# State-space scan of a two-block model: each head's decay sums are repeated on 128 partitions by transfers from DRAM instead of by selection products

## The chip, the cores and the metric

The kernel runs on one core of one Trainium2 chip. Its engines are TensorE (PE in the profile, with its weight loads as PEld), VectorE (DVE), ScalarE (ACT), GpSimd (POOL) and SyncE (SP), which here only issues DMA transfers. Sixteen DMA engines move data between DRAM and the on-chip memory SBUF; TensorE writes its results to the eight banks of PSUM. The metric is the time of one execution on the device in microseconds, as the median of several runs.

## The reference, cut to what matters

The reference computes two blocks on 512 tokens of width 1024. The first block has a state-space branch (32 heads in 4 groups, forward and backward over the sequence), a pooling branch and a mixture of 32 experts; the second has attention, a recurrence and two feed-forward layers. The change lies in the chunked scan of the first block:

```python
def step(state, inp):                      # one chunk of q = 128 tokens
    xc, ac, bc, cc = inp
    acs = jnp.cumsum(ac, axis=1)
    seg = acs[:, :, None] - acs[:, None, :]
    decay = jnp.exp(jnp.where(lower, seg, -jnp.inf))
    cb = jnp.einsum('bign,bjgn->bijg', cc, bc)
    y_diag = jnp.einsum('bijg,bijgr,bjgrp->bigrp', cb, decay, xc)
    ...
```

`acs` is the running sum of the decay within a chunk, for each of 32 heads and 2 directions. The matrix `seg` needs, for every pair of tokens (i, j) of a chunk, the sum at i minus the sum at j. The kernel holds j on the 128 partitions and i along the free dimension, for four chunks side by side (512 columns). The sum at j is then one number per partition, but the row of sums at i has to stand on all 128 partitions. How this row gets there is what is changed.

## The kernel before, in words

Every engine has its own program, written as Python functions with the engine's name in front (`pe_scan`, `act_scan`, `dve_scan`); semaphores tie them together. `x.next(key)` marks an instruction, `wait_ge(*x.when(key))` waits for it. Each engine runs its instructions in the order in which they are written out.

**Where the sums are.** `acs2` holds them with the token on the partition, each twice. TensorE transposes them (L1054 to L1060), so that row hh of the result (hh = 32 d + 8 g + h for direction d, group g, head h) holds the 512 sums of one head and direction. ScalarE copies all 128 rows to `ats` rounded to float32r (L2052), VectorE replaces the lower 64 by the rest that the rounding left (L2646, called at L2806), and ScalarE makes a table `oneh` of selection columns.

**The heads.** The scan goes through four groups of eight heads. In a group, six chunks of the input projection are made and convolved ("wxbc" weights), then four state steps run, then the eight heads one after another. `pe_decayed(g, h)` selects row hh of `ats` onto all partitions of a PSUM bank, once per direction: two matmuls of 512 columns (L1014). `act_decayed` turns the backward bank into the exponent of the decay, in four ACTIVATE instructions (L1981) written to `E4[h % 2][0]`; `dve_decayed` does it with the forward bank, in four TENSOR_SCALAR instructions (L2743) written to `E4[h % 2][1]`, and then merges the two with a copy under a mask (L2748). `act_exponential` (L1987) takes the exponential, VectorE multiplies by C·B (L2923), and TensorE multiplies with the head's inputs (L1145).

**What is woven in.** After each head, `gap(1, True)` lets two other streams go on. The `filler` is half a weight tile's products for z and the gates ("wz", "wg", later "wu"), 12 matmuls of 512 columns (L851 to L853). The result goes through `FB` to a DRAM scratch (`spill`, L1917 and L1919, 256 KB). The `later` stream is one tile of the second modulation matrix ("wada", L940), and every fourth time a turn (L950). On ScalarE the order in a head is: `act_decayed` of the next head, the exponential, and then the filler's part. That is the high half of a coming weight tile (`hi`, L502) or a spill.

**Weight tiles.** SyncE loads them, 512 KB each, into four slots (`raw`), in the order in which TensorE takes them (L460). A tile of "wz", "wg", "wxbc" or "wu" is split by ScalarE into a high part (L502) and by VectorE into a low part (L513), and its slot is free after the low part. A "wada" tile is used as it is, and its slot is free when TensorE has used it. `Plan` fixes in advance which slot each tile gets and at which point it is split, some tiles ahead of its use (AHEAD = 4). In the heads of groups 0 to 2 the order is two "wada", one "wz" or "wg", and so on. For example, the first "wada" after tile wz 11 gets the slot of wz 11, the second that of an earlier "wada".

## Time and profile before

| | |
|---|---|
| median of 3 runs | 2458.35 us (2451.48 to 2459.67) |
| the profiled execution | 2453.99 us, its span 2452.6 us |
| TensorE busy | 2379.8 us, 97% of the span |
| VectorE, ScalarE, GpSimd busy | 65%, 46%, 15% |
| chain that ended last | PE 75%, DMA 10%, DVE 8%, ACT 5% |
| SyncE's queue (q1) | 377.42 MB, 41.5% of the 16 DMA engines' time |
| ScalarE's queue (q10) | 25.17 MB, 2.8% |
| selection products (L1014) | 64, from 189.9 to 651.4 us |

The span is one execution as the hardware profiler saw it. A share is the busy time over that span, and a mean over stages that have different limits: in the expert stage (slices 16 to 22 of 40) the DMA engines are full, in the scan TensorE is. The chain is followed back from the last instruction to what released each step.

### The profile page before, as it was taken

The page shows a single profiled execution, that of the slowest core. Times are in us where ns is not written, and L with a number is a line of the kernel's source. Part 1 is how long each engine was busy: PE and PEld are TensorE (multiplying, and loading weights), DVE is VectorE, ACT ScalarE, POOL GpSimd, SP SyncE. Part 2 cuts the span into 40 slices and gives each one's busy share as a digit, 9 for nine tenths or more (in the row PEclk, how much of TensorE's full clock was granted, in tenths as well). Part 3 has the DMA queues.
Part 4 walks back from the last instruction along what each step waited for, and adds up shares of the span by engine and source line. Part 5 has one row for each costly group of instructions (what it writes and reads, how often), then busy time and mean ns, then how long its engine had stood idle before and what let it go on. Part 6 is the DMA issues. An engine that isn't in the chain of part 4 may idle for free.

```text
span 2452.6 us, 34034 instructions
## 1 busy us (share of the span) xinstructions
PE 2379.8 (97%) x13716; PEld 1913.7 (78%) x13716; DVE 1586.6 (65%) x2352; ACT 1134.8 (46%) x1690; POOL 357.8 (15%) x324
## 2 busy tenths in 40 slices
PE   6999999999899999999999989999999999999999
PEld 3876868677777877777666678989988777889988
DVE  2676676868645667655555677667753677667666
ACT  2424434343445446655555574434353546534433
POOL 0010111202232311111111110100032000201110
PEclk9999999999999999999999999999999999999999
DMA  7315234242346369999999934767542111567763
GB/s 273 116 60 182 93 126 145 87 140 96 129 154 221 119 218 384 424 423 423 423 422 423 373 130 133 168 163 185 113 144 77 44 43 52 155 147 180 174 156 109
DMA packets 127043, 467.83 MB, mean 191 GB/s; under 512 B 17194, under 2 KB 27690, under 8 KB 101153
## 3 DMA queue, kind: packets, MB, share of 16 engines
q1 hardware_dynamic: 91488, 377.42, 41.5%
q0 software_dynamic: 21952, 63.01, 12.2%
q10 hardware_dynamic: 13440, 25.17, 2.8%
q8 instruction: 110, 1.80, 0.3%
q14 instruction: 53, 0.43, 0.1%
HBM read 440.96 MB, written 31.72 MB: 193 GB/s over the span
## 4 chain that ended last, share of the span: by engine, by line
PE 75%; DMA 10%; DVE 8%; ACT 5%; issue 1%; SPq 0%; POOL 0%; ACTq 0%; DVEq 0%; POOLq 0%
PE bank L851 13%; PE bank L853 13%; PE bank L852 13%; DMA pair<-in_ed 8%; PE bank L1617 5%; PE bank L1619 5%; PE bank L1620 5%; PE bank L1443 2%; DVE HLB L513 2%; PE bank L1421 1%; PE bank L1423 1%; PE bank L1422 1%; ACT HLB L502 1%; PE bank L1493 1%; DVE HLB L306 1%
## 5 line engine op out<-in xcount | busy, mean ns | idle before, releaser
L513 DVE TENSOR_TENSOR HLB<-raw,HLB 128x1024 fp32r<-128x1024 f32 (+2 forms) x210 | 250.9, 1198 | 193.0 <-ACT HLB L502 192.3
L851 PE MATMUL bank<-HTh,HLB 128*128 128x512 f32 (+2 forms) x750 | 306.8, 409 | 14.8 <-DVE HLB L513 11.3
L853 PE MATMUL bank<-HTh,HLB 128*128 128x512 f32 (+2 forms) x750 | 291.6, 389 | 0.0
L852 PE MATMUL bank<-HTl,HLB 128*128 128x512 f32 (+2 forms) x750 | 290.7, 388 | 0.0
L502 ACT ACTIVATE HLB<-raw 128x1024 fp32r<-128x1024 f32 (+2 forms) x218 | 209.5, 968 | 121.2 <-PE bank L853 68.4
L502 ACT ACTIVATE HLB<-quad 128x1024 fp32r<-128x1024 f32 x133 | 139.0, 1056 | 146.0 <-PE bank L853 76.2
L513 DVE TENSOR_TENSOR HLB<-quad,HLB 128x1024 fp32r<-128x1024 f32 x133 | 161.2, 1220 | 61.4 <-ACT HLB L502 61.1
L851 PEld LDWEIGHTS bank<-HTh,HLB 128*128 128x128 f32 (+1 forms) x750 | 143.7, 192 | 72.4 <-issue 27.4
L1617 PE MATMUL bank<-HTh,HLB 128*128 128x256 f32 x608 | 170.0, 280 | 0.2 <-ACT tmp L2464 0.2
L1619 PE MATMUL bank<-HTl,HLB 128*128 128x256 f32 x608 | 169.8, 279 | 0.0
L1620 PE MATMUL bank<-HTh,HLB 128*128 128x256 f32 x608 | 169.7, 279 | 0.0
L853 PEld LDWEIGHTS bank<-HTh,HLB 128*128 128x128 f32 (+1 forms) x750 | 143.4, 191 | 30.5
L852 PEld LDWEIGHTS bank<-HTl,HLB 128*128 128x128 f32 (+1 forms) x750 | 143.8, 192 | 27.8 <-issue 2.2
L851 PE MATMUL bank<-FA,HLB 128*128 128x512 f32 x352 | 139.1, 395 | 1.8 <-DVE FA L2646 1.8
L853 PE MATMUL bank<-FA,HLB 128*128 128x512 f32 x352 | 138.9, 395 | 0.0
L852 PE MATMUL bank<-FA,HLB 128*128 128x512 f32 x352 | 138.9, 395 | 0.0
L1619 PE MATMUL bank<-TTl,HLB 128*128 128x256 f32 x456 | 128.3, 281 | 0.0
L1617 PE MATMUL bank<-TTh,HLB 128*128 128x256 f32 x456 | 128.3, 281 | 0.0
L1620 PE MATMUL bank<-TTh,HLB 128*128 128x256 f32 x456 | 128.2, 281 | 0.0
L306 DVE TENSOR_TENSOR HLB<-ht_pair,HLB 128x1024 fp32r<-128x1024 f32 x98 | 114.1, 1219 | 14.9 <-ACT HLB L297 14.5
L373 POOL DMA_DIRECT2D quad<-in_q x57 | 53.7, 942 | 445.1 <-DVE HLB L513 282.4
L1617 PEld LDWEIGHTS bank<-HTh,HLB 128*128 128x128 f32 x608 | 114.2, 188 | 0.7 <-issue 0.4
(671 smaller groups left out, 5902.2 us busy)
## 6 DMA issues: line engine op xcount, KB each, us to landing
quad<-in_q SPq DMA_DIRECT2D x76, 512.0 KB, 5.5
pair<-in_ed SPq DMA_DIRECT2D x32, 1024.0 KB
ht_pair<-in_eu SPq DMA_DIRECT2D x31, 1024.0 KB, 24.0
quad<-in_q POOLq DMA_DIRECT2D x57, 512.0 KB, 6.8
raw<-in_wada SPq DMA_DIRECT2D x40, 512.0 KB, 4.0
raw<-in_f SPq DMA_DIRECT2D x48, 384.0 KB, 3.4
raw<-in_eg SPq DMA_DIRECT2D x17, 1024.0 KB, 7.2
pair<-in_eu SPq DMA_DIRECT2D x17, 1024.0 KB
```

What stands on the lines that cost most here:

```text
L306: self.nc.vector.tensor_tensor(lo, raw, hi.bitcast(F32), ALU.subtract).then_inc(*self.w_lo.next(h))
L373: self.nc.gpsimd.dma_start(self.raw(name, p, BLOCK_OF[op]), source, accum_op=ALU.add).then_inc(*self.sums[self.place[(name, p, BLOCK_OF[op ...
L502: self.nc.scalar.activation(hi, raw, ACT.Copy).then_inc(*self.w_hi.next(n))
L513: self.nc.vector.tensor_tensor(lo, raw, hi.bitcast(F32), ALU.subtract).then_inc(*self.w_lo.next(n))
L851: mm(bank, ah, bh, start=(start and i == 0), stop=False)
L852: mm(bank, ah, bl, start=False, stop=False)
L853: ins = mm(bank, al, bh, start=False, stop=(stop and i == n - 1))
L1421: mm(bank[:, :], XGh[:, k, :], hi[:, kk, :], start=(k == 0), stop=False)
L1443: ins = mm(bank[64 * f:64 * f + 64, 256 * u:256 * u + 256], x, w[:, kk, 256 * f:256 * f + 256], start=(k == u == 0), stop=(k == 7 and u == 1))
L1617: mm(out, w.hi[:, n, :], xh[:, k, :], start=(start and n == 0), stop=False, skip_group_check=not start)
L1619: mm(out, w.hi[:, n, :], xl[:, k, :], start=False, stop=False, skip_group_check=not start)
L1620: ins = mm(out, w.lo[:, n, :], xh[:, k, :], start=False, stop=(n == 7), skip_group_check=not start)
```

## The change

`pe_decayed` and the table `oneh` go, and with them the 64 selection products. ScalarE copies the 64 rows of sums in full precision to `ats` and stores them in a DRAM scratch `AD` (64 x 512). For each head and direction a transfer, issued by ScalarE, then reads one row of `AD` 128 times (the source steps by zero from partition to partition) and writes it to 128 partitions, 256 KB. The forward row lands in `E4[h % 2][1]`, where VectorE then works in place; the backward row lands in `ats`, which is a single buffer. The forward transfer of head h + 2 is issued after the exponential of head h (those of heads 0 and 1 before the state steps and at the third); the backward transfer of head h + 1 is issued after ScalarE's L1981 of head h, whose own completion it waits for. What was a wait of `dve_decayed` for a free buffer is now a wait of ScalarE before it issues the transfer.

```diff
@@ -583,6 +586,7 @@
         GD = nc.dram_tensor("g_scratch", (16, 128, 512), F32, kind="Internal").ap()
         UD = nc.dram_tensor("u_scratch", (4, 128, 4, 256), F32, kind="Internal").ap()
         YZD = nc.dram_tensor("yz_scratch", (16, 128, 512), F32, kind="Internal").ap()
+        AD = nc.dram_tensor("a_scratch", (64, 512), F32, kind="Internal").ap()
         H2 = nc.dram_tensor("h2_scratch", (512, 1024), F32, kind="Internal").ap()
         YD = nc.dram_tensor("y_scratch", (1024, 1024), F32, kind="Internal").ap()
         H2_BY_HALF = H2.rearrange("(i p) (h n) -> p i h n", p=128, h=2)
@@ -619,8 +623,7 @@
         tw = place("tw", [128, 4, 64])
         etot = place("etot", [128, 4, 64])
         cw = place("cw", [128, 2, 64])
-        ats = place("ats", [128, 512], FR)
-        oneh = place("oneh", [128, 64, 1], FR)
+        ats = place("ats", [128, 512])
         DEC_END = at[0]
         W0 = at[0]
         XT = place("XT", [128, 8, 512])
@@ -1004,17 +1007,6 @@
         ORDER = [[("b", 16 + g), ("c", 20 + g)] + [("x", 4 * g + j) for j in range(4)] for g in range(4)]
         PLACE = {xc: n % 3 for n, xc in enumerate(xc for order in ORDER for _kind, xc in order)}
 
-        def pe_decayed(g, h):
-
-            for d in range(2):
-                hh = 32 * d + 8 * g + h
-                bank = psum.take(pe, ("sums", g, h, d))
-                pe.wait_ge(*dve_out.when("ats"))
-                pe.wait_ge(*act_out.when("oneh"))
-                mm(bank[:, :], oneh[:, hh, :].to_broadcast([128, 128]), ats[:, :], start=True, stop=True).then_inc(
-                    *pe_out.next(("sums", g, h, d)))
-                psum.give(("sums", g, h, d), act_out if d else dve_out, ("seg", g, h, d))
-
         AFTER = [(1, 2, 2), (1, 2, 2), (1, 2, 1), (1, 2, 1)]
 
         def pe_scan(gap):
@@ -1057,7 +1049,7 @@
             for i in range(4):
                 ins = transpose(bank[:, cols(i)], acs2[:, i, :, :].rearrange("p a b -> p (a b)"), K("ident"))
             ins.then_inc(*pe_out.next("ats"))
-            psum.give("ats", dve_out, "ats")
+            psum.give("ats", act_out, "ats")
 
             def place_chunk(kind, xc):
                 ca = CA[PLACE[xc]]
@@ -1127,14 +1119,10 @@
                                 *pe_out.next(("up", g, step, d)))
                         for d in range(2):
                             psum.give(("up", g, step, d), dve_out, ("state", g, step + 1, d))
-                    else:
-                        pe_decayed(g, 0)
                     for d in range(2):
                         psum.give(("off", g, step, d), dve_out, ("tq", g, step, d))
                     gap(1, True)
                 for h in range(8):
-                    if h < 7:
-                        pe_decayed(g, h + 1)
                     if h:
                         psum.give(("yd", g, h - 1), dve_out, ("yd", g, h - 1))
                     gap(1, True)
@@ -1967,6 +1955,26 @@
                 yield
             store(3)
 
+        def decayed_row(g, h, d):
+            hh = 32 * d + 8 * g + h
+            return AD[hh:hh + 1, :].to_broadcast([128, 512])
+
+        def act_forward(g, h):
+
+            if h == 0:
+                act.wait_ge(*pe_out.when(("state", g, 1)))
+            elif h == 1:
+                act.wait_ge(*pe_out.when(("up", g, 2, 1)))
+            else:
+                act.wait_ge(*dve_out.when(("seg", g, h - 2)))
+            nc.scalar.dma_start(E4[h % 2][1][:, :], decayed_row(g, h, 0)).then_inc(*forward_in[h % 2].next((g, h)))
+
+        def act_backward(g, h):
+
+            if h or g:
+                act.wait_ge(*act_out.when(("seg", *((g, h - 1) if h else (g - 1, 7)), 1)))
+            nc.scalar.dma_start(ats[:, :], decayed_row(g, h, 1)).then_inc(*backward_in.next((g, h)))
+
         def act_decayed(g, h):
 
             if h == 0:
@@ -1975,16 +1983,20 @@
                 act.wait_ge(*pe_out.when(("up", g, 2, 1)))
             else:
                 act.wait_ge(*pe_out.when(("yd", g, h - 2)))
-            act.wait_ge(*pe_out.when(("sums", g, h, 1)))
+            act.wait_ge(*backward_in.when((g, h)))
             hh = 32 + 8 * g + h
             for c in range(4):
-                ins = activation(E4[h % 2][0][:, cols(c)], psum[("sums", g, h, 1)][:, cols(c)], ACT.Identity, scale=-1.0,
+                ins = activation(E4[h % 2][0][:, cols(c)], ats[:, cols(c)], ACT.Identity, scale=-1.0,
                                  bias=src[:, c, hh:hh + 1])
             ins.then_inc(*act_out.next(("seg", g, h, 1)))
+            if h < 7:
+                act_backward(g, h + 1)
 
         def act_exponential(g, h):
             act.wait_ge(*dve_out.when(("seg", g, h)))
             activation(E4[h % 2][0][:, :], E4[h % 2][0][:, :], ACT.Exp, scale=-1.0).then_inc(*act_out.next(("dec", g, h)))
+            if h < 6:
+                act_forward(g, h + 2)
 
         def act_start():
             s = KM["sel"]
@@ -2049,11 +2061,9 @@
             gap(1)
             act.wait_ge(*pe_out.when("ats"))
             act.wait_ge(*consts_in.when("pr"))
-            activation(ats[:, :], psum["ats"][:, :], ACT.Copy).then_inc(*act_out.next("ats"))
-            for i in range(2):
-                p = slice(64 * i, 64 * i + 64)
-                activation(oneh[p, :, 0], km[p, KM["ident"] + 64 * i:KM["ident"] + 64 * i + 64], ACT.Copy).then_inc(
-                    *act_out.next("oneh"))
+            activation(ats[0:64, :], psum["ats"][0:64, :], ACT.Copy).then_inc(*act_out.next("ats"))
+            act.wait_ge(*act_out.now())
+            nc.scalar.dma_start(AD, ats[0:64, :]).then_inc(*sums_out.next("rows"))
 
             def place_chunk(g, kind, xc):
                 if kind == "c":
@@ -2107,9 +2117,14 @@
                     act.wait_ge(*pe_out.when(("state", g, d)))
                     activation(ST[d][:, :], psum[("state", g, d)][:, :], ACT.Copy).then_inc(
                         *act_out.next(("state", g, d)))
+                if g == 0:
+                    act.wait_ge(*sums_out.when("rows"))
+                act_forward(g, 0)
+                act_backward(g, 0)
                 for step in range(4):
                     if step == 3:
                         act_decayed(g, 0)
+                        act_forward(g, 1)
                         gap(1, True, lambda: act_exponential(g, 0))
                     else:
                         gap(1, True)
@@ -2732,15 +2747,9 @@
 
         def dve_decayed(g, h):
             hh = 8 * g + h
-            if h == 0:
-                dve.wait_ge(*pe_out.when(("state", g, 1)))
-            elif h == 1:
-                dve.wait_ge(*pe_out.when(("up", g, 2, 1)))
-            else:
-                dve.wait_ge(*dve_out.when(("seg", g, h - 2)))
-            dve.wait_ge(*pe_out.when(("sums", g, h, 0)))
+            dve.wait_ge(*forward_in[h % 2].when((g, h)))
             for c in range(4):
-                ins = tensor_scalar(E4[h % 2][1][:, cols(c)], psum[("sums", g, h, 0)][:, cols(c)],
+                ins = tensor_scalar(E4[h % 2][1][:, cols(c)], E4[h % 2][1][:, cols(c)],
                                     src[:, c, hh:hh + 1], -1.0, ALU.subtract, ALU.mult)
             ins.then_inc(*dve_out.next(("seg", g, h, 0)))
             dve.wait_ge(*dve_out.now())
@@ -2802,8 +2811,6 @@
             dve.wait_ge(*act_out.when("eacs"))
             tensor_tensor(cw[:, :, :], cw[:, :, :], dec[:, 4:6, :], ALU.mult).then_inc(*dve_out.next("co"))
             gap(1)
-            dve.wait_ge(*act_out.when("ats"))
-            rest(ats[64:128, :], psum["ats"][64:128, :], ats[64:128, :], "ats")
 
             def place_chunk(g, kind, xc):
                 if g:
```

## Rows read from the trace of the kernel before

**Rows 1.** Busy time by stretch (TensorE alone): us, busy (instructions), clock, DMA share, GB/s

```profile
325.00:372.00 47.00, 47.00 (x270) 1.00 0.45 156
469.00:512.00 43.00, 39.40 (x206) 0.96 0.44 153
```

**Rows 2.** The same view, at the end of group 0's heads

```profile
230.00:232.00 2.00, 0.00 (x0) 1.00 0.24 98
234.00:236.00 2.00, 2.00 (x12) 0.55 0.58 229
```

**Rows 3.** The chain of waits, 180 to 660 us, end of group 0: start, us, what

```profile
220.69 0.53 PE bank L1014 x2
221.30 1.15 ACT tmp L1981 x4
222.54 0.75 DVE tmp L2748
...
223.95 0.96 ACT HLB L502
224.93 1.23 DVE HLB L513
226.18 3.68 DMA raw<-in_wxbc
```

**Rows 4.** Timeline of SyncE's queue, group 0: start, us, line, transfer, count

```profile
197.47 0.88 SPq L460 DMA_DIRECT2D raw<-in_wada  x2
...
206.77 0.88 SPq L460 DMA_DIRECT2D raw<-in_wada  x2
207.70 0.47 SPq L460 DMA_DIRECT2D raw<-in_wz  x1
216.29 0.88 SPq L460 DMA_DIRECT2D raw<-in_wada  x2
```

**Rows 5.** Landings of L460's loads, issues of 207.6 to 208, then 217.15 to 218

```profile
DMA to landing us min/median/max: 5.5/5.9/6.2
...
DMA to landing us min/median/max: 4.7/5.1/5.5
```

**Rows 6.** Timeline of ScalarE, group 0: idle time before it in brackets

```profile
213.95 1.06 ACT L502 ACTIVATE HLB<-raw 128x1024 fp32r<-128x1024 f32 x1 [0.53 <-DMA raw<-in_wz]
```

**Rows 7.** Busy time by stretch, all engines (PE, PEld, DVE, ACT, POOL), within one round

```profile
210.50:211.50 1.00, 1.00 (x11) 0.54 (x11) 1.00 (x5) 0.73 (x3) 0.00 (x0) 1.00 1.06 404
214.50:215.50 1.00, 1.00 (x11) 1.00 (x11) 0.46 (x1) 0.51 (x1) 0.00 (x0) 1.00 0.00 0
```

**Rows 8.** Landing of L1919's spill of 256 KB, issued in 210 to 211

```profile
DMA to landing us min/median/max: 4.2/4.2/4.2
```

**Rows 9.** Timeline of ScalarE's queue, then the DMA issues (KB each, us to landing)

```profile
210.34 0.33 ACTq L1919 DMA_DIRECT2D z_scratch<-FB  x1
...
RA<-z_scratch ACTq DMA_DIRECT2D x8, 256.0 KB, 3.3
```

**Rows 10.** Groups of instructions by line and shape, VectorE: busy us, mean ns, idle before

```profile
L2743 DVE TENSOR_SCALAR tmp<-bank,src 128x128 f32<-128x128 f32 x128 | 35.8, 341 | 9.0 <-PE bank L1014 9.0
...
L3750 DVE TENSOR_SCALAR tmp<-tmp,ms 128x128 f32<-128x128 f32 x6 | 1.7, 286 | 0.2
```

**Rows 11.** Timeline of SyncE's queue, group 1

```profile
346.59 0.88 SPq L460 DMA_DIRECT2D raw<-in_wada  x2
...
366.28 0.37 SPq L460 DMA_DIRECT2D raw<-in_wada  x1
```

**Rows 12.** The chain of waits, group 2's last heads

```profile
489.59 4.74 DMA raw<-in_wg
...
497.08 5.87 DMA raw<-in_wxbc
```

**Rows 13.** The chain of waits, group 3's heads

```profile
641.86 1.05 ACT HLB L502
...
647.14 1.05 ACT HLB L502
```

More of the change, by code:

```diff
@@ L539, in build @@
         sel_in = signal("sel_in", 16)
+        sums_out = signal("sums_out", 16)
+        forward_in = [signal(f"forward_in{i}", 16) for i in range(2)]
+        backward_in = signal("backward_in", 16)
         q_load = [signal(f"q_load{i}", 16) for i in range(6)]
```

## The prediction

> **What bounds the kernel now.** I read the page first (TensorE busy 97% of the span), then the busy time by stretch, then the chain of waits through the scan, then SyncE's queue and the landings of its loads. The change touches 190 to 651 us alone, in four stretches of eight heads (groups 0 to 3). In the heads of group 1 TensorE is busy 47.00 of 47 us, in those of group 2 39.40 of 43 [rows 1]. So TensorE looks like the bound, and work taken from it like time won. But at the end of group 0 it stands still: no matmul in 230 to 232 [rows 2]. The chain there shows why [rows 3]: TensorE's pair of selection products, ScalarE's L1981, ScalarE's high part of a weight tile (L502), VectorE's low part (L513), then a load of 3.68 us, then L502 again.
>
> SyncE shows that this is a loop [rows 4]. Per two heads it issues two "wada" tiles and one "wz" or "wg" tile, of 512 KB each, and it can do so only when the tile before is split, since the first "wada" goes into its slot. One round is 0.93 us from the first issue to the third, the landing, 1.09 for the high part and its hand-over, and 1.24 for the low part. The third tile landed 6.2 us after its issue in the second round [rows 5], and 0.93 + 6.2 + 1.09 + 1.24 = 9.5, against a measured 216.29 - 206.77 = 9.52. L502 stood waiting for that tile for 0.53 us [rows 6]. So the loads' round and TensorE's two heads (9.8 us) run side by side, with less than a microsecond between them. In the third round the tile (issued 0.93 after 216.29) landed 5.5 after its issue [rows 5]: 222.7, and L502 began at 223.95 [rows 3], 1.2 later; this floor is 8.8 against 9.89.
>
> During such a round the 16 DMA engines are full: share 1.06 and 404 GB/s in 210.5 to 211.5, and 0.00 in 214.5 to 215.5 [rows 7]. A burst, then a pause.
>
> **What the change does, part by part.**
>
> 1. It removes 32 pairs of selection products (64 matmuls L1014). On the chain a pair costs 0.53 us [rows 3]; 32 x 0.53 = 17.0 us of TensorE. This is the most that can be won, if TensorE alone set the ends of the stretches.
>
> 2. It adds 64 transfers of 256 KB from DRAM, two per head, 16.8 MB: 2 x 0.262 MB in 4.9 us is 107 GB/s on top. At 404 GB/s [rows 7] each takes the engines 0.65 us. The trace has a direct case of such a transfer inside a burst: the spill of 256 KB issued at 210.34 landed after 4.2 us [rows 8], and the tile of that burst came 6.2 after its issue against 5.5 in the next burst, into which its spill came later [rows 5]. The difference, 0.7, is about the 0.65. In ScalarE's order four of the new transfers are issued per round, about one every 2.4 us; a burst takes 7.1 us (0.93 + 6.2), the last one comes near its end, so three count: 3 x 0.65 = 2.0 us per round. The ends are 0 (all fall in the pause) and 2.6 (all four). I take 2.0, nearest to the spill's case.
>
> 3. ScalarE issues them, 0.33 us each [rows 9], two per head. The backward one follows L1981; ScalarE would then wait for VectorE's L2748 anyway (0.75 us [rows 3]), so it costs nothing. The forward one follows the exponential, just before L502: 0.33 on the chain where that chain is ScalarE and VectorE alone, nothing where L502 waits for a load. VectorE's L2743 reads SBUF in place of PSUM: 286 against 341 ns at 128x128 [rows 10], four per head, 0.22 us less. I take ScalarE's L1981 as unchanged (it also changes to SBUF); a tenth either way per instruction would be 0.4 per head on an engine busy 46% of the span.
>
> 4. The new waits. VectorE's for the forward row is harmless: it is issued almost two heads ahead (after the exponential of head h, for h+2). The backward row has one buffer: L1981, 1.15 us [rows 3], its completion and the issue, the landing, then the next L1981. Reads of 256 KB from scratch land after 3.3 us [rows 9]: 1.15 + 0.1 + 3.3 = 4.6 us per head, less than a head of 4.9. In a burst, with the 4.2 of the spill [rows 8], it is 5.5. Behind ScalarE's waiting instruction stand the exponential and L502, and for these VectorE and SyncE wait. With rounds of 11.5 us (5.75 per head) it stays just inside.
>
> 5. The store of the sums (128 KB), the smaller copy L2052, two copies and L2646 that go: all near 100 us, with 80 us before the first use. Nothing. Eight PSUM banks now serve half as many takers; TensorE waits for none today, so nothing.
>
> The sum, by group. Before the first round two pairs fall away ahead of the split: -1.0. *Group 0*: floors 9.3 (the first round took that), 9.5 and 8.8, 27.6 in all, each plus 2.0, is 33.6, against the measured 226.18 - 197.47 = 28.7 [rows 3, 4]: +4.9 - 1.0 = +3.9. After the last round the load of the convolution's weights is issued at once and TensorE waits for it [rows 2, 3], so all of this reaches the next stage. *Group 1*: from 346.59 to 366.28 are two rounds, 19.7 us [rows 11]; L502 waits for neither tile, so I give them group 0's floors with a tile at 6.2 and at 5.5, 9.5 + 8.8 = 18.3, plus 4.0 is 22.3: +2.6; TensorE's pairs ahead of them give back 1.0: +1.6. *Group 2*: the chain from 485 on holds two loads, 4.74 and 5.87 [rows 12], with fewer transfers beside each (the heads are longer there, about 7 us): +1.3 and +1.0. Four forward issues on the chain, +1.3, four faster L2743, -0.9, and the pairs before 485, -1.0: +1.7. *Group 3*: no tile waits for a load; ScalarE and VectorE hand tiles to each other, 5.28 us from one L502 to the next [rows 13]. Five such heads at 0.33 - 0.22 = +0.1 each, with the pairs at its start (-0.5): 0. Sum: 3.9 + 1.6 + 1.7 + 0 = +7.2. After the stand at 230 TensorE's granted clock was 0.55 in 234 to 236, most of it at 1.2 GHz [rows 2]; longer stands add perhaps 0.5 to 1 of that. I take +8.
>
> The profiled execution took 2453.99 us (span 2452.6 and 1.4 around it); it becomes 2462. The median of the three runs before is 2458.35, 4.4 higher, so the forecast on the median's footing is 2466.5.
>
> By the Trainium skill ("DMA: Bandwidth & Descriptors", section "Queues, rings and completion order") each DMA engine alternates between SyncE's and ScalarE's rings packet by packet, so a transfer that comes late in a burst still takes its share at once. By that rule n = 3 or 4 and the sum stands or rises to about +12. Were a late transfer served behind what is queued, two would count, 1.3 a round, and the sum would be +4; the spill's 4.2 us leaves both open.
>
> **The rivals.**
>
> A. *The pauses take the transfers* (17%). The engines are idle some 3 of 9.5 us [rows 7]. For it: mean share in the heads is under one half. Against it: ScalarE issues a backward row just as each burst begins. Nothing is added to the rounds: group 0 is 27.6 - 28.7 - 1.0 = -2.1, group 1 18.3 - 19.7 - 1.0 = -2.4, group 2 -0.6, group 3 0: -5.1, so 2453.
>
> B. *TensorE alone sets the ends* (5%). This is the other side: the loop of loads has hidden slack (a slot more than I count), and the whole pair is won, from the first head on. -17.0: 2441. It decides if L502 can come later without moving TensorE; the stand at 230 speaks against it.
>
> C. *The single backward buffer sets the head* (10%). In a burst the new row shares the engines with three tiles, not with the end of one. If it lands after 5.0 us, L1981's cycle is 1.15 + 0.1 + 5.0 = 6.25 per head, beyond the rounds' 5.75: 0.5 more in each of 14 heads of groups 0 and 1, +7 beside the sum's +8: 2469. For it: one buffer, and ScalarE's order puts L502 behind. Against it: half of the rows fall into a pause.
>
> D. *Reading one row 128 times is slow* (18%). All 16 engines read the same 2 KB. No row of this trace does so. If a transfer then holds the engines twice as long, 1.3 us, the round grows by 4.0: group 0 +9.9, group 1 +5.6, group 2 +4.0, group 3 +1 (the backward cycle, 1.15 + 0.1 + 4.0, comes to its 5.28): +20.5, with the half clock +22, so 2480. At four times it would be some +60. Beside it stands what the Trainium skill says ("DMA: Bandwidth & Descriptors", section "Latency and other measured facts"): rows spaced by large powers of two fell from about 207 to 103 GB/s, by inference because they meet in few channels of HBM. One row read by all would be the extreme of that; no run here shows it yet.
>
> **How the numbers follow.** The forecast (50%) has 2461 to 2472 as its own range (1.3 to 2.6 us a round). What a measurement of this kernel can tell from no change is about 0.3%, 7.4 us: 2451.0 to 2465.7. Slower by more: over half of the forecast (0.28), nearly all of D (0.17), half of C (0.05): 0.50. Faster by more: B and a part of A (0.08): 0.13. The rest, 0.37, is the same. The range that leaves out a fifth goes from A's upper part, 2452, to beyond D, 2492.
>
> **What would show it.** In the profile after: no L1014; TensorE's busy time down by some 17 to 28 us and its idle time in the heads up by more; the third tile's landing in the bursts of group 0 near 8 us in place of 6; L502's waits for "wz", "wg" and "wxbc" up from under 19 us in the scan to over 30; SyncE's rounds at 11 to 12 us; the share of ScalarE's queue up by some 16.8 MB, at the time per byte that it has now (D: twice that). Right in direction but wrong in reason would be a wait of L1981 for the backward row that comes ahead of L502's (C). The prediction is wrong if the rounds stay at 9.5 us with the new transfers beside them (A), or if group 0 ends before 224 us.

## The result, and the profile after

The changed kernel takes 2469.6 us (median of 7 runs, 2466.0 to 2472.9); the kernel before, beside it on the same chip, took 2456.1 (7 runs). The ratio is 1.0065, 95% interval [1.0054, 1.0076]. That is slower by 14 us (the medians) to 16 (the ratio), where 64 products of TensorE went away. The forecast was +8 us. The profiled executions are 15.7 us apart (spans 2468.3 and 2452.6), so they can be compared directly.

The page of the kernel after: its busy time, then ScalarE's DMA queue (packets, MB, share of 16 engines), then the chain that ended last.

```profile
PE 2377.2 (96%) x13652; PEld 1914.5 (78%) x13652; DVE 1580.1 (64%) x2351; ACT 1139.8 (46%) x1688; POOL 356.4 (14%) x324
q10 hardware_dynamic: 22736, 42.09, 5.1%
PE 71%; DMA 14%; DVE 9%; ACT 5%; issue 1%; SPq 0%; ACTq 0%; POOL 0%; DVEq 0%; POOLq 0%
```

The same two lines of the kernel before:

```profile
PE 2379.8 (97%) x13716; PEld 1913.7 (78%) x13716; DVE 1586.6 (65%) x2352; ACT 1134.8 (46%) x1690; POOL 357.8 (15%) x324
q10 hardware_dynamic: 13440, 25.17, 2.8%
```

TensorE has exactly 64 matmuls fewer, and yet its busy time fell by 2.6 us only. The queue carries 16.92 MB more, and its packets took 57 us of 16 engines more (5.1% of 2468.3 less 2.8% of 2452.6). That is 366 GB/s for the old ones, and 296 for the new, if the old kept their pace.

Where the time went, by stage. The table has the start of ScalarE's first backward instruction (L1981, after: L1989) of one head, in the span's time:

| start of | before | after | later by |
|---|---|---|---|
| group 0, head 0 | 191.0 | 188.2 | -2.8 |
| group 0, head 7 | 230.8 | 236.3 | +5.5 |
| group 1, head 7 | 373.3 | 384.0 | +10.7 |
| group 2, head 7 | 519.9 | 531.3 | +11.3 |
| group 3, head 7 | 653.3 | 668.9 | +15.6 |

All of it is lost inside the scan. ScalarE can run behind TensorE for a while, so what reaches the next stage is better read from TensorE's own product for a head (L1145, after: L1133). For the first head of groups 1, 2 and 3 it starts 5.9, 7.5 and 10.2 us later than before, and for the last head of group 3 15.4.

Now SyncE's queue in group 0, which answers to [rows 4] (start, us, line, transfer, count):

```profile
194.92 0.88 SPq L460 DMA_DIRECT2D raw<-in_wada  x2
195.85 0.87 SPq L460 DMA_DIRECT2D raw<-in_wz  x1
207.33 0.88 SPq L460 DMA_DIRECT2D raw<-in_wada  x2
208.25 0.47 SPq L460 DMA_DIRECT2D raw<-in_wz  x1
219.30 0.88 SPq L460 DMA_DIRECT2D raw<-in_wada  x2
...
231.42 0.82 SPq L460 DMA_DIRECT2D raw<-in_wxbc  x2
```

A round of loads grew from 9.3, 9.5 and 9.9 us to 12.4, 12.0 and 12.1. The "wz" tiles landed 9.1, 8.7 and 7.1 us after their issue; in [rows 5] the two that stand there took 6.2 and 5.5. The DMA issues of 190 to 232 us (KB each, median us to landing) name the new neighbours:

```profile
raw<-in_wada SPq DMA_DIRECT2D x6, 512.0 KB, 6.7
tmp<-a_scratch ACTq DMA_DIRECT2D x7, 256.0 KB, 4.8
ats<-a_scratch ACTq DMA_DIRECT2D x6, 256.0 KB, 4.9
raw<-in_wz SPq DMA_DIRECT2D x3, 512.0 KB, 8.7
```

In the kernel before, the same view of 192 to 228 us:

```profile
raw<-in_wada SPq DMA_DIRECT2D x6, 512.0 KB, 4.3
raw<-in_wz SPq DMA_DIRECT2D x3, 512.0 KB, 6.0
```

The chain of waits through group 0 (start, us, what) no longer goes by the tiles, as it did in [rows 3], but up to 227 us by the backward rows, head after head:

```profile
201.48 4.60 DMA ats<-a_scratch
...
206.17 1.29 ACT tmp L1989 x4
207.46 0.02 issue
207.48 6.24 DMA ats<-a_scratch
213.75 0.05 issue
213.80 1.29 ACT tmp L1989 x4
215.09 0.02 issue
215.11 3.61 DMA ats<-a_scratch
...
220.11 5.92 DMA ats<-a_scratch
```

That is the loop of the single backward buffer: four instructions in 1.29 us, then the landing, before the next four may start. And the stands of TensorE have a second price. By stretch (us, then busy time and instructions of PE, PEld, DVE, ACT, POOL, then the granted clock, DMA share, GB/s), inside the second round after:

```profile
204.00:207.00 3.00, 1.47 (x7) 0.87 (x5) 0.93 (x1) 1.89 (x4) 0.00 (x0) 1.00 0.42 145
207.30:208.30 1.00, 0.34 (x3) 0.35 (x4) 1.00 (x5) 0.15 (x1) 0.00 (x0) 1.00 0.00 0
208.30:215.30 7.00, 7.00 (x26) 5.11 (x26) 3.01 (x10) 2.39 (x6) 0.00 (x0) 0.51 0.90 290
```

TensorE was idle for 1.5 of 3 us and then for 0.66 of one, and the granted clock of the next 7 us is 0.51, its level of 1.2 GHz. The work there counts as busy, but takes longer: a product of L855 stands in the chain for 0.43 us at 242 us (granted clock 0.51) and for 0.23 at 185 (1.00). This is where the busy time that the products gave back went. The mean granted clock fell from 0.990 to 0.985; in e3 below, where it stays at 0.992, TensorE's busy time does fall, by 18.9 us.

### The profile page after: what moved, and what is told of

It is laid out like the page before. It is cut to its first block, busy times and chain, and to the rows that moved or that the text cites. A ratio compares the mean times of both kernels' runs of the same rounds, so it can differ in the third digit from the quotient of the medians.

```text
span 2468.3 us, 33945 instructions
## 1 busy us (share of the span) xinstructions
PE 2377.2 (96%) x13652; PEld 1914.5 (78%) x13652; DVE 1580.1 (64%) x2351; ACT 1139.8 (46%) x1688; POOL 356.4 (14%) x324
## 4 chain that ended last, share of the span: by engine, by line
PE 71%; DMA 14%; DVE 9%; ACT 5%; issue 1%; SPq 0%; ACTq 0%; POOL 0%; DVEq 0%; POOLq 0%
PE bank L854 12%; PE bank L856 12%; PE bank L855 12%; DMA pair<-in_ed 8%; PE bank L1605 5%; PE bank L1607 5%; PE bank L1608 5%; DMA ats<-a_scratch 2%; PE bank L1431 2%; DVE HLB L513 2%; DVE HLB L306 2%; PE bank L1409 1%; ACT HLB L502 1%; PE bank L1411 1%; PE bank L1410 1%; DMA ht_pair<-in_eg 1%
## 5 line engine op out<-in xcount | busy, mean ns | idle before, releaser
L854 PE MATMUL bank<-HTh,HLB 128*128 128x512 f32 (+2 forms) x750 | 311.1, 415 | 15.3 <-DVE HLB L513 10.9
L856 PE MATMUL bank<-HTh,HLB 128*128 128x512 f32 (+2 forms) x750 | 294.5, 393 | 0.0
L855 PE MATMUL bank<-HTl,HLB 128*128 128x512 f32 (+2 forms) x750 | 294.4, 393 | 0.0
L502 ACT ACTIVATE HLB<-raw 128x1024 fp32r<-128x1024 f32 (+2 forms) x218 | 209.8, 969 | 132.8 <-PE bank L856 68.4
L502 ACT ACTIVATE HLB<-quad 128x1024 fp32r<-128x1024 f32 x133 | 139.1, 1056 | 145.1 <-PE bank L856 76.2
L855 PEld LDWEIGHTS bank<-HTl,HLB 128*128 128x128 f32 (+1 forms) x750 | 146.1, 195 | 27.6 <-issue 1.7
L855 PE MATMUL bank<-FA,HLB 128*128 128x512 f32 x352 | 138.9, 395 | 0.0
## 6 DMA issues: line engine op xcount, KB each, us to landing
raw<-in_f SPq DMA_DIRECT2D x48, 384.0 KB, 3.3
```

The costliest lines, as they stand in the source:

```text
L502: self.nc.scalar.activation(hi, raw, ACT.Copy).then_inc(*self.w_hi.next(n))
L854: mm(bank, ah, bh, start=(start and i == 0), stop=False)
L855: mm(bank, ah, bl, start=False, stop=False)
L856: ins = mm(bank, al, bh, start=False, stop=(stop and i == n - 1))
```

## The experiments

The theories at the start: *loads' round* (the new transfers hold up the tiles that share a burst), priced by bytes (in the expectations also L, or B for bytes); *C*, the single backward buffer sets the head (B in e1 and e5); *D*, the same row read by 128 partitions is slow. Later come *R*, a price by the number of rows that a transfer writes, and *T*, a price for each transfer on ScalarE's queue. All ratios are to the kernel before, run beside the changed ones.

**e1: a second backward buffer.** The rows alternate between two buffers and are asked for two heads ahead.

```
-            nc.scalar.dma_start(ats[:, :], decayed_row(g, h, 1))...
+            nc.scalar.dma_start(BACK[h % 2][:, :], decayed_row(g, h, 1))...    # BACK = [ats, RA]
...
-            if h < 7: act_backward(g, h + 1)
+            if h < 6: act_backward(g, h + 2)
```

> The changed kernel with a second buffer for the backward row (it lies free during the heads), so that the row for head h+2 is asked for after ScalarE's work on head h, two heads ahead like the forward row. Theory B (the single backward buffer sets the head: ScalarE's cycle is 1.29 us plus a landing of 3.6 to 6.2): the waits of ScalarE's four instructions for that row (31.9 us in the changed kernel) go to under 5, the heads of groups 0 to 2 get about 1 us shorter each, the time falls by 6 to 12 us against the changed kernel, to 2458 to 2464. Theory L (the weight loads' round is longer by the new bytes, 3 us for each tile, and would hold the heads at 12 us per two anyway): the waits move from the row to L502's tiles and the time stays within 3 us of 2469.6.

Measured: 2463.5 us, ratio 1.0043 [1.0030, 1.0056]. What ScalarE's backward instructions waited for in 185 to 660 us, first in the kernel after (L1989), then here (L1992):

```profile
  DMA ats<-a_scratch: 29.7, 17
  ACT FB L1905: 2.5, 6
  PE bank L1133: 1.3, 1
```

```profile
  ACT FB L1906: 6.9, 15
  PE bank L944: 1.4, 3
```

29.7 us of waits for the backward rows are gone, and the kernel won 5 to 6. In groups 0 and 1 nothing was won: head 7 of group 1 starts 10.9 us later than before (after: 10.7), for the rounds of loads remained (12.6, 11.9 and 12.3 us, "wz" landing after 9.3, 8.6 and 9.0). The two loops had grown to nearly the same length, and the rounds hid what the buffer cost. In groups 2 and 3 the buffer had been the bound: the lag there fell from +11.3 and +15.6 to +6.9 and +6.1.

**e2: each partition reads a row of its own.** As e1, with the sums stored 128 times; a transfer has the same bytes and rows, but no two partitions read one place.

```
-        AD = nc.dram_tensor("a_scratch", (64, 512), F32, ...)
+        AD = nc.dram_tensor("a_scratch", (64, 128, 512), F32, ...)
-            nc.scalar.dma_start(AD, ats[0:64, :])...
+            nc.scalar.dma_start(AD, ats[0:64, :].unsqueeze(1).to_broadcast([64, 128, 512]))...
```

> The kernel with two backward buffers, but the sums are stored in DRAM 128 times each (16.8 MB, written near 100 us, which delays the stages before the heads), so that each partition reads a row of its own. It is looked at for the landings in the heads alone. Rival D of the prediction (128 reads of one row are slow): the rows' landings fall from a median of 4.6 to 5.1 us to 3.5 or less, and the tiles' with them. If the place that is read does not matter: the same landings within 0.5 us.

Measured: 2461.8 us in one run, span 2460.5. That looks like no gain over e1 (span 2461.2), but the store of 16.8 MB has its own price ahead of the scan: the first head starts at 201.9 us instead of 188.4. From there to the last head's start e2 takes 459.1 us, and e1 takes 471.0. Rows of their own are worth 12 us of the scan. The landings, for which the run was made, fell too: in 190 to 232 us, against e1's, "wada" from 7.0 to 4.7 us, "wz" from 9.0 to 7.0, and the backward rows from 5.6 and 5.5 to 4.2 and 3.2, one of the two under the 3.5 that was expected. I count this as shown only together with e9, which has no such side effect.

**e3: nearly all of the transfers gone.** Each group fetches one pair of rows, and all of its heads use the first head's decay: 8 transfers instead of 64, and no products.

```
-            nc.scalar.dma_start(E4[h % 2][1][:, :], decayed_row(g, h, 0))...
+            if h == 0:
+                nc.scalar.dma_start(RA[:, :], decayed_row(g, 0, 0))...
```

> The changed kernel with one pair of transfers per group (8 in all, for its first head) instead of eight pairs: every head of a group uses the decay of that head, so 56 of the 64 transfers and their issues and waits are left out, and no selection product is made. It shows what taking the products from TensorE is worth alone. If TensorE sets the ends of the heads: 17 us under the kernel before, 2439. If the loads' round (9.3, 9.5 and 8.8 us in group 0) sets them, as the prediction had it: 3 to 7 us under, 2449 to 2453.

Measured: 2440.9 us, ratio 0.9952 [0.9939, 0.9965]. Rounds are back at 10.0, 9.8 and 8.9 us, "wz" at 6.5, 6.5 and 5.5. So the products were worth 12 us of the 17 that they fill, and the transfers, with their issues and waits, cost 28 (1.0065 against 0.9952). The loss is the transfers', all of it. The 3 to 7 us that went with the prediction were too few: the time came within 2 us of what was set for TensorE as the bound.

**e4 and e6: fewer bytes, or fewer rows.** From e3's footing, the other 56 transfers come back cut down: e4 moves 16 columns of 128 partitions (8 KB), e6 all columns of 16 partitions (32 KB). The heads still use the first head's decay.

```
e4: nc.scalar.dma_start(ats[:, 0:16], decayed_row(g, 0, 1)[:, 0:16])...
e6: nc.scalar.dma_start(ats[0:16, :], decayed_row(g, 0, 1)[0:16, :])...
```

> As the kernel with one pair per group, but the other 56 transfers are issued and waited for with 16 columns each (64 bytes per partition, 8 KB) in place of 512: all issues and waits of the changed kernel, nearly none of its bytes; every head of a group uses the decay of its first head. If the bytes on the DMA engines are the cost (they lengthen both the rows' own landing and the weights'): landings near 2 us, no waits, and within 3 us of the kernel with one pair per group. If issue time and the fixed part of the landing are the cost, it stays at 2460 or above.

> As the kernel with short transfers (56 of 64 transfers carry data that nobody needs, every head of a group uses the decay of its first head), but each of the 56 is 16 partitions by 512 columns (32 KB in 16 rows) in place of 128 partitions by 16 columns (8 KB in 128 rows). Four times the bytes, an eighth of the rows, as many transfers, issues and waits. In the short kernel the weight tile of group 0 landed 8.2 us after its issue though the new bytes were nearly none. Theory R (a transfer costs by its rows, one descriptor each, which ScalarE's and SyncE's queues get one after the other): tiles land near 6 us again, the rows near 2, and the time is within 4 us of the kernel with one pair, 2441 to 2446. Theory T (each transfer on ScalarE's queue costs by itself): it stays at 2458 to 2464.

Measured: e4 2461.9 us, ratio 1.0038 [1.0025, 1.0050]; e6 2450.7, ratio 0.9987 [0.9974, 0.9999]. With one thirty-second of the bytes e4 keeps three quarters of the cost: 0.0086 above e3, where all of it is 0.0113. e6 moves four times e4's bytes and costs 0.0035. The price by bytes has failed here. e6 falls between the ranges of R and T, and a look by groups says why. From TensorE's first head product to that of group 1's last head, e3 takes 181.1 us, e6 180.9 and e4 191.9. From there to the last head of group 3 they take 268.1, 274.7 and 274.4. So in groups 0 and 1 the 16 reads of e6 cost nothing and e4's 128 cost 11 us. In groups 2 and 3 both cost about 6; the single buffer and the issues, which both have and e3 hasn't, would fit that, but e9 below has both too and pays 3 only. What remains for groups 0 and 1 is the number of reads, or the address that they share.

**e5: forward rows by transfer, backward rows by products.** One transfer and one product per head.

```
+            for d in (1,):      # pe_decayed: the backward product alone
...
-            act.wait_ge(*backward_in.when((g, h)))
+            act.wait_ge(*pe_out.when(("sums", g, h, 1)))
```

> The kernel before with the forward rows by transfer and the backward rows still by selection products: half the bytes, half of TensorE's saving, and no single buffer, since the forward row is asked for two heads ahead. Theory B: nothing waits for a row; 8.5 us of products gone, some given back by the bytes, 2450 to 2456. Theory L: rounds longer by 1 to 1.5 us in groups 0 and 1, 2458 to 2463.

Measured: 2452.0 us, ratio 0.9991 [0.9980, 1.0002]. Half of the change costs nothing and brings nothing; the loss came with the second half, which also brings the single buffer. If half of the products is worth half of e3's 12 us, these 32 transfers cost some 5, and the cost isn't proportional to the number of transfers.

**e7: GpSimd issues the rows.** As e1, with the 64 transfers in GpSimd's queue.

```
-            nc.scalar.dma_start(BACK[h % 2][:, :], decayed_row(g, h, 1))...
+            nc.gpsimd.dma_start(BACK[h % 2][:, :], decayed_row(g, h, 1))...
```

> The kernel with two backward buffers, all 64 full transfers issued by GpSimd in place of ScalarE, at the same waits (GpSimd's own queue, descriptors made in software). If what the transfers cost lies in the making of descriptors shared by SyncE's and ScalarE's queues (theories R and T): the tiles' landings fall to between 6.5 and 8 us, with 64 issues of 0.33 us gone from ScalarE, 2448 to 2458. If the cost is the DMA engines' own (bytes or rows in their rings, theory L in its first form): no change against the kernel with two buffers, 2461 to 2466.

Measured: 2466.7 us, ratio 1.0051 [1.0036, 1.0067], against e1's 1.0043: no difference that can be told from the scatter. The rows land after 5.8 to 6.3 us, the first "wz" after 12.2. The issuing engine isn't the cause. The Trainium skill says so too ("DMA: Bandwidth & Descriptors", section "Issuing engines are not separate DMA queues"): whoever issues, the same 16 engines do the work. This case agrees.

**e8: one transfer per head.** The head's forward and backward sums lie side by side in DRAM, and one transfer gives each partition one run of 4 KB, into one of two buffers of 1024 columns. The bytes are those of the changed kernel; the reads are half as many.

```
-        AD = nc.dram_tensor("a_scratch", (64, 512), F32, ...)
+        AD = nc.dram_tensor("a_scratch", (32, 2, 512), F32, ...)
+            row = AD[8 * g + h:8 * g + h + 1].rearrange("h d n -> h (d n)")
+            nc.scalar.dma_start(BOTH[h % 2][:, :], row.to_broadcast([128, 1024]))...
```

> Both rows of a head adjacent in DRAM and in a buffer of 1024 columns (two such, free during the heads): one transfer of 128 rows of 4 KB per head in place of two of 2 KB. The same bytes, half the rows, transfers and issues; asked for two heads ahead. Theories R and T: the tiles land 1 to 1.5 us sooner than in the kernel with two buffers, 2451 to 2458. If bytes are what costs: 2461 to 2465.

Measured: 2446.4 us, ratio 0.9971 [0.9961, 0.9980]: faster than both kernels, and by more than either theory had set. The DMA issues of 190 to 228 us, of e8:

```profile
raw<-in_wada SPq DMA_DIRECT2D x6, 512.0 KB, 4.2
YZP<-a_scratch ACTq DMA_DIRECT2D x3, 512.0 KB, 4.6
raw<-in_wz SPq DMA_DIRECT2D x3, 512.0 KB, 7.0
ASP<-a_scratch ACTq DMA_DIRECT2D x3, 512.0 KB, 6.5
```

512 KB land about as soon as 256 KB did in e1 (5.5 to 6.0), and the "wada" tiles are as quick as before the change; the "wz" tiles still land 1 us later. At equal bytes, and two buffers for the backward row in both, e8 is 17 us faster than e1. One thing more differs: in the first round e1 issues a row at 195.07, 0.1 us before SyncE's first load; e8 issues its first one at 197.10, 2.2 us behind that load, and the start of the burst has none beside it.

**e9: the small transfers, each partition from its own place.** e4 again; the one difference in the scan is the address. Partition p reads its 64 bytes 2 KB behind those of partition p - 1, where in e4 all 128 read the same 64 bytes.

```
-            row = decayed_row(g, 0, 1)[:, 0:16]      # e4: stride 0 over the partitions
+            row = AC[32 + 8 * g][:, 0:16]            # AC: (64, 128, 512), filled once
```

> As e4_short, but each partition of a small transfer reads its 64 bytes from a place of its own in DRAM, 2 KB from the next one, where e4 read the same 64 bytes 128 times. Every head uses the decay of its group's first head, as in e4. Theory R (a transfer costs its neighbours by its number of rows, whatever they hold and wherever they come from): as e4, the weights' tiles land after 7.9 to 8.3 us in the first group's heads, median 2458 to 2465. Theory D (reading one address from all partitions is the slow thing): the tiles land after 6.0 to 6.9 us, median 2441 to 2452.

Measured: 2446.0 us, ratio 0.9978 [0.9968, 0.9988], against e4's 1.0038. The view of DMA issues in 190 to 232 us, e4 and then e9:

```profile
raw<-in_wada SPq DMA_DIRECT2D x6, 512.0 KB, 6.8
raw<-in_wz SPq DMA_DIRECT2D x3, 512.0 KB, 8.1
ats<-a_scratch ACTq DMA_DIRECT2D x7, 8.0 KB, 3.6
```

```profile
raw<-in_wada SPq DMA_DIRECT2D x6, 512.0 KB, 4.7
raw<-in_wz SPq DMA_DIRECT2D x3, 512.0 KB, 6.4
ats<-c_scratch ACTq DMA_DIRECT2D x7, 8.0 KB, 2.5
```

Same bytes, same rows, same program order; the tiles beside them are about 2 us sooner. The start of the first round shows how. By stretch, from the second microsecond after SyncE's first issue, e4 and then e9:

```profile
198.80:199.80 1.00, 1.00 (x8) 0.88 (x7) 0.96 (x4) 0.00 (x0) 0.00 (x0) 1.00 0.07 5
199.80:200.80 1.00, 1.00 (x14) 0.65 (x13) 0.30 (x2) 0.76 (x2) 0.00 (x0) 1.00 0.48 150
200.80:201.80 1.00, 1.00 (x8) 0.73 (x5) 1.00 (x4) 0.36 (x1) 0.00 (x0) 1.00 0.77 216
201.80:202.80 1.00, 1.00 (x6) 0.83 (x5) 0.39 (x2) 0.00 (x0) 0.00 (x0) 1.00 0.94 304
202.80:203.80 1.00, 1.00 (x6) 0.80 (x5) 0.00 (x0) 0.73 (x3) 0.00 (x0) 1.00 1.06 418
```

```profile
196.80:197.80 1.00, 1.00 (x8) 0.88 (x7) 0.96 (x4) 0.00 (x0) 0.00 (x0) 1.00 0.43 97
197.80:198.80 1.00, 1.00 (x14) 0.65 (x13) 0.30 (x2) 0.78 (x2) 0.00 (x0) 1.00 1.03 391
198.80:199.80 1.00, 1.00 (x8) 0.74 (x5) 1.00 (x4) 0.54 (x2) 0.00 (x0) 1.00 1.04 393
```

The last two columns are the DMA share and GB/s. TensorE and VectorE do the same work in the first three stretches of both. In e9 the burst is at full rate in the third microsecond after the issue; in e4, in the sixth. The lost time is no packet's. In 190 to 232 us the 2592 packets of q10 take 9.2% in e4, and the 2505 in e9 8.5%, some 24 and 23 ns each.

At 256 KB it is the same. The third and fourth microseconds of a round, e1 (first round) and then e2 (second round):

```profile
197.20:198.20 1.00, 1.00 (x14) 0.59 (x12) 0.30 (x2) 0.81 (x2) 0.00 (x0) 1.00 0.69 125
198.20:199.20 1.00, 1.00 (x8) 0.79 (x5) 1.00 (x4) 0.54 (x2) 0.00 (x0) 1.00 0.93 268
```

```profile
210.70:211.70 1.00, 1.00 (x14) 0.61 (x13) 0.30 (x2) 0.80 (x2) 0.00 (x0) 1.00 1.04 373
211.70:212.70 1.00, 1.00 (x8) 0.77 (x5) 1.00 (x4) 0.54 (x2) 0.00 (x0) 1.00 1.04 397
```

e6, with 16 reads of one address, has no such slow start either (377 GB/s in 197.8 to 198.8, the third microsecond).

**e10, e11, e12: fewer rows in the tiles themselves.** "w_ada" is laid out so that each partition of a tile gets one run of 4 KB, not two of 2 KB: in e8, in the kernel before, and in the changed kernel.

```
-         return w[:, 2 * key[2]:2 * key[2] + 2, c * 512:(c + 1) * 512]
+         return w[:, c, 2 * key[2]:2 * key[2] + 2, :]
```

> e8_one_per_head with the tiles of w_ada laid out in DRAM so that each of a tile's 128 partitions gets one run of 4 KB instead of two of 2 KB: half the rows in those transfers, the same bytes. Theory R (by rows): the tiles that share the burst land 0.5 to 1.5 us sooner in every round that sets the end, median 2438 to 2444. Theory B (a full burst goes by its bytes): no change from e8, 2444 to 2449.

> The kernel before, with the same layout of w_ada. Theory R: the tiles wz and wg land after 5.0 to 5.7 us instead of 5.5 to 6.2, median 2444 to 2452. Theory B: as before, within 3 us of it.

> The changed kernel with the same layout of w_ada. Theory R: a round of loads falls from 12 to about 11 us, median 2458 to 2465. Theory B: within 3 us of the changed kernel. The head's cycle by the single backward buffer, 1.29 + about 5 us of landing, holds by either and bounds the gain.

Measured: e10 2444.0 us, ratio 0.9968 [0.9956, 0.9980]; e11 2451.8, 0.9997 [0.9987, 1.0006]; e12 2471.7, 1.0076 [1.0064, 1.0089]. Each interval overlaps that of the kernel that it was made from (e11's holds 1). So the number of rows in these tiles is worth no time that can be measured. It isn't without effect: in 190 to 232 us the "wz" tiles' median landing fell from 6.0 to 5.3 us (before, e11), from 8.7 to 7.8 (after, e12) and from 7.0 to 6.8 (e8, e10), but the rounds did not get shorter by it in e12 (12.0, 12.3 and 12.4 us). e12 lies clear above R's range; e11's and e10's medians lie at the edge of it, so these two speak against R less strongly. e10 has the lowest median of the kernels that compute every head's decay, but it can't be told from e8.

## Why the prediction was right, and where it was not

*The bound.* Right for groups 0 and 1: the loop of loads stood under one microsecond beside TensorE, and it was what grew, so rivals A (nothing added) and B (all 17 us won) fall. What TensorE's relief is worth was put too low. Without the transfers (e3) the rounds are 10.0, 9.8 and 8.9 us, and the gain is 12 us, where rival A's terms for just that give 5.1. By TensorE's first product in each next group, the gain by group is 2.4, 5.1, 3.3 and 0.4, against 2.1, 2.4, 0.6 and 0: group 0 is right, and groups 1 and 2 leaned on the loads less than was thought.

*The sum.* The forecast +8 is 5 of gain and 13 of cost; measured were 12 of gain and 28 of cost. Both terms came out more than twice as large, and they have opposite signs, so the range held in part by luck. So did the absolute time, 2466.5 against 2469.6: the three runs that it stood on had a median of 2458.35, and the seven have 2456.05.

*The size, by the term that was mis-sized.* A transfer was priced by its bytes, 0.65 us, three per round, 2.0 us. Measured: the three rounds grew by 3.1, 2.5 and 2.2 us, and the smaller part of that is bytes. (They also began 2.6 us earlier than before, where the sum had 1.0.) The table has the stretch from the first head's start to the last head's on ScalarE, and two stretches by TensorE's product for a head: from the first head to the last of group 1, and from there to the last of group 3. All are of the profiled executions.

| kernel | transfers | scan, us | groups 0, 1 | groups 2, 3 |
|---|---|---|---|---|
| e3 | 8 | 452.7 | 181.1 | 268.1 |
| e9 | 64, of them 56 of 8 KB, own addresses, one buffer | 455.6 | 180.2 | 271.2 |
| e6 | 64, of them 56 of 32 KB, 16 reads of one address, one buffer | 457.9 | 180.9 | 274.7 |
| e2 | 64 of 256 KB, own addresses, two buffers | 459.1 | 187.0 | 268.4 |
| e8 | 32 of 512 KB, one address, two buffers | 459.4 | 187.3 | 268.4 |
| before | none, products | 462.3 | 183.9 | 275.0 |
| e4 | 64, of them 56 of 8 KB, one address, one buffer | 470.2 | 191.9 | 274.4 |
| e1 | 64 of 256 KB, one address, two buffers | 471.0 | 196.8 | 270.7 |
| after | 64 of 256 KB, one address, one buffer | 480.7 | 195.6 | 281.3 |

In groups 0 and 1, own addresses against one address: 11.7 us at 8 KB (e9, e4) and 9.8 at 256 KB (e2, e1). Thirty-two times the bytes: 6.8 us with own addresses (e9, e2), 4.9 with one (e4, e1). The bytes were the smaller part, and the address that all 128 partitions read the larger one. In groups 2 and 3 the buffer comes in: e1 takes 10.6 us less than the changed kernel. (One execution of another kernel of the same speed can differ by several us here: e10 took 453.3 for the scan and 181.8 in groups 0 and 1, e8 459.4 and 187.3. e4 against e9 stands on the medians too, 2461.9 and 2446.0; e2 against e1, and the price of the bytes, stand on single executions.)

*Rival D* was therefore true in kind, with 18% given to it. But its test was badly chosen. It said that the time per byte of ScalarE's queue would double; it rose by a quarter (296 for 366 GB/s), and e9 and e4 show that the queue's packets don't carry this cost. The delay appears in the landings of the neighbours.

*Rival C and part 4.* "It stays just inside" failed, and what the prediction named as right in direction but wrong in reason is there: L1989 waits 29.7 us for backward rows, and the chain through group 0 goes by them. (C's 2469 is counted from the profiled execution; on the footing of the other forecasts it is 2473.) The four instructions take 1.29 us, not 1.15, and the backward rows landed after a median of 4.9 us in group 0, not 4.2: four heads from 200.2 to 226.4 us are 6.55 each, over the 5.75 that was set against it. In groups 0 and 1 that cost nothing that e1 shows, since the rounds had grown to 6.0 to 6.2 per head. In groups 2 and 3, for which the sum took no such loop, it cost 9.5 of the 15.6 us of lag in the profile, and 5 to 6 us by the medians. So the wrong reason holds for some 0.4 of the loss by the medians, and 0.6 in the profiled executions.

*By group.* Forecast +3.9, +1.6, +1.7 and 0; measured +5.9, +1.6, +2.7 and +5.1, by TensorE's first product in the next group and the last one of group 3. Group 1's agreement is luck: its gain and its cost were both put too low (e3). Group 3's +5.1 is the buffer's: in e1 it is +0.4. The half clock was given up to 1 us, and no run parts it from the rest; TensorE's busy time, forecast to fall by 17 to 28, fell by 2.6. L502's waits for its tiles rose from 18.7 to 24.4 us, not over 30: the waiting moved to L1989. The part on VectorE held in sign only: the median of its instruction fell from 341 to 281 ns, but some took up to 1300, and the mean fell from 341 to 322.

The measured 14 to 16 us are inside the range, and the forecast of +8 is half of them: bytes were the wrong unit for this transfer, the buffer's loop was checked in the stages where it was hidden, not in those where it was not, and the products' own worth was put at less than half.

*Open.* Why one address costs so much isn't settled. Requests that meet at one place in the memory would fit; no run here looks inside. A price that sets in somewhere between 16 and 128 reads of one address would fit groups 0 and 1 of e6 and e4. But e8, with 128 reads of one address, takes there what e2 takes with addresses of its own (187.3 and 187.0 us). Whether e8 is quick by its fewer transfers, by its longer runs, or because none is issued right ahead of the loads, isn't told apart. Nor was a kernel run with full rows, own addresses and one buffer, which would show what the buffer costs beside short rounds.

## What to carry to other kernels

Before a transfer is set beside a burst of loads, ask what it does to the landings of its neighbours; its bytes and its own landing don't tell. Here a row that many partitions need was better fetched in one long run per head (e8), or from a place of its own for each (e2), than in two short ones from the same place. A buffer for it must be checked in every stage by instruction time plus landing under load, also where another loop now hides it. When two loops have nearly the same length, taking one away shows nothing (e1 in groups 0 and 1): judge each with the other removed. And when a gain and a cost are added, look at each with the other taken out (e3); their sum can be right where both are wrong.

## What was not expected of the hardware

- 56 transfers of 8 KB, of which every partition reads the same 64 bytes, cost 21 us with their issues and waits (e4 against e3); from addresses of their own 6 us (e9 against e3). The tiles of 512 KB beside them land after 6.8 and 4.7 us.
- Reads 2 KB apart in DRAM (e9, e2) showed no such slowness. The Trainium skill ("DMA: Bandwidth & Descriptors", section "Latency and other measured facts") gives 207 GB/s for copies at a row pitch of 512 KB and less at larger powers of two, down to 103 at 4 MB; no run here has such a pitch. The same place read by all, which the prediction took for the extreme of that rule, is what this case shows to be slow.
- 512 KB with runs of 4 KB per partition landed after 4.6 and 6.5 us (medians of two buffers, e8), where 256 KB with runs of 2 KB took 5.5 to 6.0 (e1).
- 56 transfers with 16 reads of one address (e6) cost nothing in groups 0 and 1 (180.9 us against e3's 181.1); 56 with 128 reads cost 11 us there (e4, 191.9).
- TensorE's idle 1.5 us in 204 to 207 us and 0.66 in 207.3 to 208.3 were followed by 7 us at a granted clock of 0.51.
